# Expert slot lists from indicator products on TensorE, with the token table kept for overflow slots

## The reference, cut to what matters

```python
scores = jax.nn.sigmoid((t @ w_router).astype(jnp.float32))
_, eidx = lax.top_k(scores + router_bias.astype(jnp.float32), TOP_K_EXPERTS)   # 8 of 64 experts
g = jnp.take_along_axis(scores, eidx, axis=1)
g = g / jnp.sum(g, axis=-1, keepdims=True) * ROUTED_SCALE
...
def expert_block(args):
    e, toks, gs = args
    xb = t[toks]
    return swiglu(xb, w1[e], w3[e], w2[e]) * gs[:, None]
...
shared = swiglu(t, ws1, ws3, ws2)
return (routed + shared).reshape(B, S, D)
```

## Time and profile before

| | |
|---|---|
| median of 3 runs | 2526.91 us |
| profiled execution | 2550.12 us |
| its span | 2548.3 us |
| PE busy | 2292.6 us (90%) |
| DVE busy | 1565.9 us (61%) |
| ACT busy | 1190.4 us (47%) |
| POOL busy | 289.9 us (11%) |
| mean granted clock of PE | 0.949 of full speed |

### The profile page before, as it was taken

How to read it: one execution, slowest core, us unless ns; L and a number is a source line. 1 busy time by engine, 2 the same in 40 slices (tenths; PEclk the granted TensorE clock), 3 DMA queues, 4 the chain that set the end, 5 groups by cost and what they waited for, 6 DMA issues and landing times.

```text
span 2548.3 us, 31998 instructions
## 1 busy us (share of the span) xinstructions
PE 2292.6 (90%) x10228; PEld 1779.6 (70%) x10228; DVE 1565.9 (61%) x2404; ACT 1190.4 (47%) x1774; POOL 289.9 (11%) x345
## 2 busy tenths in 40 slices
PE   6998999399999999995399989999979878999997
PEld 4776677277777777774375768887868646888875
DVE  6789654489888888886765553332453566433334
ACT  4422433088888888884134433322231573333322
POOL 0000003322332332323400000000000000000000
PEclk8999997699999999998599999999999989999999
DMA  7521133399999999996520122223212101222222
GB/s 305 195 100 58 42 131 95 77 337 380 375 355 373 375 356 355 354 345 231 204 99 25 59 68 97 99 94 104 100 66 99 42 1 66 99 91 98 99 100 83
DMA packets 124602, 422.63 MB, mean 166 GB/s; under 512 B 21024, under 2 KB 21152, under 8 KB 124384
## 3 DMA queue, kind: packets, MB, share of 16 engines
q1 hardware_dynamic: 98176, 367.86, 40.6%
q0 software_dynamic: 25376, 50.66, 5.4%
q10 hardware_dynamic: 960, 2.97, 0.3%
HBM read 419.68 MB, written 39.47 MB: 180 GB/s over the span
## 4 chain that ended last, share of the span: by engine, by line
PE 59%; DMA 15%; DVE 12%; issue 5%; ACT 4%; DVEq 1%; POOL 1%; another core or an unknown queue 0%; SPq 0%; ACTq 0%; POOLq 0%
PE PS L283 17%; PE PS L285 16%; PE PS L284 16%; DMA eraw<-wstream 14%; DVE wl L191 3%; PE PS L628 3%; ACT wh L186 2%; PE PS L650 2%; POOL YG L2276 1%; PE PS L639 1%; DMA ada_w<-wada 1%; DVEq L1188 1%; DVE M L1185 1%; DVE X L555 1%; DVE X L559 1%
## 5 line engine op out<-in xcount | busy, mean ns | idle before, releaser
L191 DVE TENSOR_TENSOR wl<-raw,wh 128x1024 fp32r<-128x1024 f32 x239 | 292.6, 1225 | 402.9 <-ACT wh L186 389.8
L283 PE MATMUL PS<-HTh,wh 128*128 128x512 f32 x1248 | 503.4, 403 | 39.4 <-DVE HTl L581 18.7
L191 DVE TENSOR_TENSOR wl<-eraw,wh 128x1024 fp32r<-128x1024 f32 x384 | 460.1, 1225 | 82.8 <-ACT wh L186 72.1
L284 PE MATMUL PS<-HTl,wh 128*128 128x512 f32 x1248 | 491.4, 394 | 0.7 <-issue 0.7
L285 PE MATMUL PS<-HTh,wl 128*128 128x512 f32 x1248 | 491.3, 394 | 0.3 <-issue 0.3
L186 ACT ACTIVATE wh<-eraw 128x1024 fp32r<-128x1024 f32 x384 | 392.1, 1053 | 106.0 <-DMA eraw<-wstream 80.0
L186 ACT ACTIVATE wh<-raw 128x1024 fp32r<-128x1024 f32 x239 | 251.7, 1056 | 393.7 <-PE PS L285 371.4
L283 PEld LDWEIGHTS PS<-HTh,wh 128*128 128x128 f32 x1248 | 237.9, 191 | 105.3 <-issue 35.6
L284 PEld LDWEIGHTS PS<-HTl,wh 128*128 128x128 f32 x1248 | 238.1, 191 | 51.2 <-issue 3.8
L285 PEld LDWEIGHTS PS<-HTh,wl 128*128 128x128 f32 x1248 | 237.6, 190 | 51.7 <-issue 0.5
L283 PE MATMUL PS<-wh,XTh 128*128 128x512 f32 x536 | 223.0, 416 | 5.4 <-DVE XTl L1873 2.4
(11 more groups left out here) (403 smaller groups left out, 3491.9 us busy)
## 6 DMA issues: line engine op xcount, KB each, us to landing
eraw<-wstream SPq DMA_DIRECT2D x192, 1024.0 KB
raw<-wstream SPq DMA_DIRECT2D x240, 512.0 KB, 3.2
ada_w<-wada SPq DMA_DIRECT2D x24, 512.0 KB, 4.3
eraw<-wexp SPq DMA_DIRECT2D x9, 1024.0 KB
ada_wb<-wada SPq DMA_DIRECT2D x2, 2048.0 KB, 15.9
ada_g<-wada SPq DMA_DIRECT2D x2, 2048.0 KB, 10.6
X<-xT SPq DMA_DIRECT2D x4, 512.0 KB, 8.2
ada_w<-wada SPq DMA_DIRECT2D x1, 2048.0 KB, 23.7
```

The source lines that it names most:

```text
L191: nc.vector.tensor_tensor(wl[:, ci % RING, :], src, wh[:, ci % RING, :].bitcast(F32), ALU.subtract).then_inc(split_done, 1)
L283: nc.tensor.matmul(o, lh, rh, start=start, stop=False)
L284: nc.tensor.matmul(o, lh, rl, start=False, stop=False)
```

## The change

The slot lists of the first 128 slots of every expert no longer come from the table in memory. For each token block and choice, DVE builds two indicator matrices: `HOTS`, which is 1 where the token's rank in its expert is the slot number, and `HOTE`, which is 1 where the column is its expert, times the token number less 512. 32 matmuls on PE sum `HOTS` transposed times `HOTE` in PSUM, so that each slot of each expert holds its token number less 512, and 0 where it is empty. This work is hung between the chunks of the shared expert (`hot` after the second and third, `lists_pe` after the fourth, `lists_dve` and `list_rows` after the fifth and sixth), and `more_counts` and `more_blocks_of` move one chunk later.

The table remains for slots beyond 128. The scatters write only those: for all others the place is set beyond the table (`NOROW`), and a bounds check leaves them out. POOL issues the 32 scatters after the gathers of experts 0 to 3 and before that of expert 4; it reads the table back in step 0 and the list of blocks in step 1. DVE and PE turn it in steps 2 and 3. The 32 gate steps are spread over steps 0 to 3 and 60 to 63, four in each. SP no longer waits for the lists before it loads chunks 8 to 11, but for `more_blocks_of`.

The diff, cut to its core:

```diff
+            TOKM = place("TOKM", [P, NB], 11064)
+            R8 = place("R8", [P, NB, 8], 11072)
+            E8 = place("E8", [P, NB, 8], 11104)
+            RSB = place("RSB", [P, E], 11136)
+            LF = place("LF", [P, E], 11200)
+            SLOT = place("SLOT", [P, P], 20032)
+            HOTE = place("HOTE", [P, NB, 8, E], 8192)
+            HOTS = place("HOTS", [P, NB, 8, P], 4096)
+            TI2 = nc.alloc_sbuf_tensor_at("TI2", [P, 2, P], I32, offset=RSTD_AT)
+            TF2 = nc.alloc_sbuf_tensor_at("TF2", [P, 256], F32, offset=RSTD_AT + 4 * 256)
...
+                nc.vector.tensor_scalar(E8[:], POS8[:], 1.0 / S, -(S / 2 + 0.5) / S, ALU.mult, ALU.add)
                 dve.wait_ge(sem("ranks"), 2)
...
+                nc.vector.tensor_scalar(E8[:], R8[:], float(P), NOROW, ALU.is_le, ALU.mult)
+                dve.drain()
+                nc.vector.tensor_tensor(E8[:], E8[:], POS8[:], ALU.add)
+                dve.drain()
+                nc.vector.tensor_scalar(POSI[:], E8[:].rearrange("p a b -> p (a b)"), -1.0, None,
+                                        ALU.add).then_inc(sem("places"), 1)
+            def hot(dve, tbs):
+                dve.wait_ge(sem("h2_out"), 16)
+                for tb in tbs:
+                    nc.vector.tensor_tensor(HOTE[:, tb, :, :], POS[:, tb, :].unsqueeze(1).broadcast_to([P, 8, E]),
+                                            POS8[:, tb, :].unsqueeze(2).broadcast_to([P, 8, E]), ALU.is_equal)
+                    nc.vector.tensor_tensor(HOTS[:, tb, :, :], SLOT[:].unsqueeze(1).broadcast_to([P, 8, P]),
+                                            R8[:, tb, :].unsqueeze(2).broadcast_to([P, 8, P]), ALU.is_equal)
+                    dve.drain()
+                    nc.vector.tensor_scalar(HOTE[:, tb, :, :], HOTE[:, tb, :, :], TOKM[:, tb:tb + 1], None, ALU.mult)
+                    dve.drain().then_inc(sem("hot"), 1)
+            def lists_dve(dve):
+                dve.wait_ge(sem("listed"), 1)
+                nc.vector.tensor_scalar(slots(IDX)[:, :, 0], PS[:, 2, 0:E], float(S), None, ALU.add)
+                nc.vector.tensor_copy(LF[:], PS[:, 2, 0:E])
+                dve.drain().then_inc(sem("lists"), 1)
...
+            def list_rows(dve):
+                nc.vector.tensor_scalar(LF[:], LF[:], 0.0, NOROW, ALU.is_ge, ALU.mult)
+                dve.drain()
+                nc.vector.tensor_tensor(LF[:], LF[:], const("rows").rearrange("p (e r) -> p e r", r=4)[:, :, 0], ALU.add)
+                dve.drain()
+                nc.vector.tensor_tensor(LF[:], LF[:], RSB[:], ALU.add)
+                dve.drain()
+                nc.vector.tensor_copy(slots(YIX)[:, :, 0], LF[:])
+                dve.drain().then_inc(sem("lists"), 1)
...
-            def gate_places(dve):
...
+            def gate_place(dve, n):
+                tb, k = n // 8, n % 8
+                nc.vector.scalar_tensor_tensor(out=LF[:], in0=SCO[:, tb, :], scalar=POSC8[:, tb, k:k + 1],
+                                               in1=G[:, tb, :], op0=ALU.is_equal, op1=ALU.mult,
+                                               accum_out=GK[:, tb, k:k + 1])
+                dve.drain()
             @stage("pool")
             def _(pool):
                 pool.wait_ge(sem("empty"), 1)
                 pool.dma_start(table.rearrange("(p s) o -> p (s o)", p=P), TI[:].rearrange("p a b -> p (a b)")).then_inc(sem("table_dma"), 16)
                 pool.wait_ge(sem("table_dma"), 16)
+                pool.wait_ge(sem("h2_out"), 16)
+            def table_scatter(pool):
                 pool.wait_ge(sem("places"), 1)
                 for tb in range(NB):
                     for k in range(8):
                         pool.indirect_dma_start(
                             out=table, out_offset=bass.IndirectOffsetOnAxis(ap=POSI[:, tb * 8 + k:tb * 8 + k + 1], axis=0),
-                            in_=TOK[:, tb:tb + 1], in_offset=None).then_inc(sem("table_dma"), 16)
+                            in_=TOK[:, tb:tb + 1], in_offset=None, bounds_check=E * S - 1,
+                            oob_is_err=False).then_inc(sem("table_dma"), 16)
+            def table_back(pool):
                 pool.wait_ge(sem("table_dma"), 16 + 16 * NB * 8)
-                pool.dma_start(TI[:], table.rearrange("(a p s) o -> p a (s o)", p=P, s=P)).then_inc(sem("table_dma"), 16)
+                pool.dma_start(TI2[:], table.rearrange("(a p s) o -> p a (s o)", p=P, s=P)).then_inc(sem("table_dma"), 16)
+            def blocks_back(pool):
                 pool.wait_ge(sem("blocks"), 1)
                 pool.dma_start(blocks, TBI[:]).then_inc(sem("blocks_dma"), 16)
                 pool.wait_ge(sem("blocks_dma"), 16)
                 pool.dma_start(TB[0:1, :], blocks[0:36, :].rearrange("(o p) c -> o (p c)", o=1)).then_inc(sem("blocks_dma"), 16)
-                pool.wait_ge(sem("h2_out"), 16)
+            def table_pe(pe):
...
+                pe.wait_ge(sem("table_f"), 1)
+                for a in range(2):
+                    mm = nc.tensor.transpose(PS[:, 5, a * P:(a + 1) * P], TF2[:, a * P:(a + 1) * P], const("ident"))
+                mm.then_inc(sem("table_t"), 1)
...
+            def table_dve(dve):
+                dve.wait_ge(sem("table_t"), 1)
+                nc.vector.tensor_copy(slots(IDX)[:, :, 1:4], PS[:, 5, 0:256].rearrange("p (e r) -> p e r", r=4)[:, :, 1:4]
+                                      ).then_inc(sem("places"), 1)
+                nc.vector.tensor_scalar(TF2[:], PS[:, 5, 0:256], float(S), NOROW, ALU.is_ge, ALU.mult)
+                dve.drain()
+                nc.vector.tensor_tensor(TF2[:], TF2[:], const("rows"), ALU.add)
+                dve.drain()
+                for r in range(1, 4):
+                    v = slots(TF2)[:, :, r]
+                    nc.vector.tensor_tensor(v, v, RSB[:], ALU.add)
+                dve.drain()
+                nc.vector.tensor_copy(slots(YIX)[:, :, 1:4], slots(TF2)[:, :, 1:4]).then_inc(sem("places"), 1)
...
+                    hot(dve, (0, 1))
+                if c == 2:
+                    hot(dve, (2, 3))
                     more_counts(dve)
+                if c == 4:
+                    lists_dve(dve)
+                    more_blocks_of(dve)
+                if c == 5:
+                    list_rows(dve)
+            def lists_pe(pe):
+                for tb in range(NB):
+                    pe.wait_ge(sem("hot"), tb + 1)
+                    for k in range(8):
+                        mm = nc.tensor.matmul(PS[:, 2, 0:E], HOTS[:, tb, k, :], HOTE[:, tb, k, :],
+                                              start=tb + k == 0, stop=tb + k == NB + 6)
+                mm.then_inc(sem("listed"), 1)
+            def shared_pe(pe, c):
                 if c == 3:
-                    more_blocks_of(dve)
-
-            def shared_pe(pe, c):
-                if c == 2:
+                    lists_pe(pe)
+                if c == 3:
...
-            @stage("dve")
-            def _(dve):
-                gate_places(dve)
...
-            @stage("pe")
...
             @stage("sp")
             def _(sp):
-                sp.wait_ge(sem("places"), 3)
+                sp.wait_ge(sem("table_dma"), 16)
+                sp.wait_ge(sem("blocks"), 1)
                 for j in range(8, ER, 2):
...
+                    if n == 3:
+                        table_pe(pe)
                 steps(pe, prologue, step)
...
+                    if n == 2:
+                        dve.wait_ge(sem("table_dma"), 32 + 16 * NB * 8)
+                        nc.vector.tensor_copy(TF2[:], TI2[:].rearrange("p a b -> p (a b)")).then_inc(sem("table_f"), 1)
+                    if n == 3:
+                        table_dve(dve)
+                    if n < 4 or n >= E - 4:
+                        for j in range(4):
+                            gate_place(dve, 4 * (n if n < 4 else n + 8 - E) + j)
...
-                    pool.wait_ge(sem("places"), 2)
+                    pool.wait_ge(sem("lists"), 1)
                     for n in range(4):
+                        pool.wait_ge(h2_low, hl0 + 2 * n + 2)
                         gather(pool, n, 0)
-                    pool.wait_ge(sem("places"), 3)
+                    table_scatter(pool)
+                    pool.wait_ge(sem("lists"), 2)
                 def step(n, i):
                     if n + 4 < E:
                         gather(pool, n + 4, i)
                     elif n + 2 < E:
                         p = n + 4 - E
+                        pool.wait_ge(sem("places"), 3)
                         more_gather(pool, p, pool.value_load(TB[0:1, 3 * p + 1:3 * p + 2], min_val=0, max_val=255))
                     scatter(pool, n, i)
+                    if n == 0:
+                        table_back(pool)
+                    if n == 1:
+                        blocks_back(pool)
                 steps(pool, prologue, step)
```

More of the change, by code:

```diff
@@ L128, in build @@
         rstd = sb("rstd", [P, S])
+        RSTD_AT = nc.sbuf_base - 4 * S
         lamc = sb("lamc", [P, 8])
```

(58 more changed lines are left out.)

5 lines of the change are left out of this document (4 added, 1 removed).

## The result

The changed kernel takes 2539.16 us (median of 5 runs, 2531.67 to 2539.86) against 2526.18 (5 runs): ratio 1.0041, interval 1.0029 to 1.0052, 7 to 13 us slower. The forecast of 2535 had side and size, but its terms did not all come out: two errors of opposite sign nearly cancelled, which is luck.

What follows compares the result with a forecast made beforehand. Expert steps taken as bound by the weight stream, before 590 us by PE. Stream +3.6, following experts +3, tail +1.5 gave +8.1, 2535 us; range 2527 to 2543, widened to 2511 to 2545.

Steps and rivals of the forecast that it cites:

- Which time to sum against: Whole kernel: the 21.8 us of late signals belong to the profiled execution; timed runs have the first expert matmul near 490.0.
- rival of real late signals: Shared expert: late signals are real and vanish with the scatter, 21.8 us saved, 2513 us; chance 0.22.
- Shared expert: Shared expert: down product at 460.0, 6.2 us later than 453.8; list products hidden beside DVE's work.
- What that gain is: Before the experts: the gates' 11.7 us are gone; first expert matmul 10.4 us before 490.0.
- Scatters on POOL: POOL, between gathers 3 and 4: 32 scatters slowed by DVE's splits; gather 4 issued at 523.6.
- U: First expert matmul on PE: forecast at 479.6 us in the changed kernel, 490.0 in the kernel before.
- The conflict with VectorE: POOL's scatters in expert steps: DVE splits of two SBUF operands block them, ending 8.8 us later than without conflict.
- the first sentence that was taken from the Trainium skill: SBUF access: a VectorE instruction with two SBUF inputs and a GpSimd instruction reading SBUF block each other whole.
- the page's inference about descriptor generation: POOL's scatters: such a VectorE instruction leaves descriptor generation alone; by this the scatters end 8.8 us sooner.
- PE's stand: Step 2, before expert 4's transposes: PE stands 22 us for its gather, landing 6.5 us after issue.
- Stream: Weight stream in expert steps: +3.6 us from a full ring, then +3 (0 to 5) over five experts.
- Tail: Last four expert steps: gates need 1.5 us per step on DVE with 1.3 free; +1.5 us.

Runs made afterwards that it cites:

- second profile of the kernel before: The kernel before, unchanged, profiled once more: 2527.71 us.
- The gates alone: Kernel before with only the gate products moved, four to a step, into steps 0 to 3 and 60 to 63: 2529.91 us, ratio 1.0007.
- the two copies: Scatters before gathers 0 to 3, looped gates, chunks 8 to 11 first, plus two PSUM copies ahead of VectorE's last splits: 2516.91 us, ratio 0.9955.
- first profile of the kernel before: The kernel before, unchanged, the profile the prediction was made from: 2550.12 us.
- the scatters early: Changed kernel with the 32 table scatters back in front of POOL's gathers 0 to 3: 2524.9 us, ratio 0.9981.
- the gates are in the loop too: Changed kernel with scatters before gathers 0 to 3 and gate products one per step in steps 4 to 59: 2521.31 us, ratio 0.9963.
- moved to the loop: Gate products one per step in steps 4 to 59: in the changed kernel 2532.32 us; with scatters before gathers 0 to 3 as well, 2521.31 us.

## Why the prediction came out as it did

- **Which time to sum against: right, and it decided the side.** 490.0 was forecast for the first expert matmul in timed runs, 491.77 measured; silu and AFs came within 1.1 us of the forecast, the end of the shared expert 1.6 us behind it (467.0, 465.4). The rival of real late signals is out.
- **Shared expert: 1.4 us short.** The down product was to come 6.2 us later than before, at 460.0; it came at 462.67, 9.2 us later than in the second profile of the kernel before (453.45), and 1.6 of these were there at the shared expert's first matmul (426.80, 428.42). The 32 list products take 7.25 us, within the 4.1 to 7.8 bounded, but stand in PE's queue ahead of the down product until 462.31; and VectorE's next split ran at 458.92, not 456.4, so AHl was done at 462.26. Both end together, so the products cost nothing beside VectorE's work, as forecast. First expert matmul 482.39 against 479.6; the gain to there 9.4 us against 10.4, or 10.9 without the 1.5 us that were there at 384 us.
- **What that gain is: wrongly named.** I wrote that the gates' 11.7 us are gone. The gates alone, taken away, gave nothing at expert 0; it is the scatters' landing and the read-back that left the path.
- **Scatters on POOL: right in place, the time partly by luck.** Forecast: gather 4 issued at U + 44, 523.6; measured 521.90. U itself came 2.8 us later than forecast, so this is U + 39.5: the 32 scatters took 47.8 us (473.01 to 520.82), where the forecast had 51.7. The conflict with VectorE is there (0.98 to 1.97 us; shown by itself by the two copies), though no scatter took over 2 us, where several over 3 were forecast. The trace agrees with the first sentence that was taken from the Trainium skill (SBUF — State Buffer, "Who interferes with whom"), and not with the page's inference about descriptor generation.
- **PE's stand: 12.3 us, 22 forecast.** The gather landed 3.4 us after its issue, not 6.5: by then the stream had stopped (DMA share 0.16), a case for which the earlier trace rows has no row. And PE wanted it at 512.98, U + 30.6, not U + 28.5: 1.5 us had been taken off for the low clock at the start of the experts, but the changed kernel starts there too (0.63 to 0.67 us a matmul until 486 us, granted clock 0.83 from 480 to 490). The step of 9.4 us is right, but not from the rows named for it: 507.50 to 541.87 in four gives 8.6, and 9.4 is the distance from the third expert's transposes on (523.13 to 541.87 in two).
- **Stream: too dear.** +3.6 and +3 forecast; at expert 63 the changed kernel is 1.9 us behind, 0.4 if the 1.5 us of 384 us are taken off, 4.0 against the first profile of the kernel before set back by its 20.0 us at expert 0. All three are less than 6.6. It is 8.5 us ahead at expert 0, 2.2 behind after the hole, 7.8 behind at expert 7, 4.7 at 22 and 1.9 at 63: the stream makes up most of it. Of the way from expert 4 to 7 the forecast had next to nothing; gates were put "beside PE's stall", but those of steps 2 and 3 and the table lie behind it. With the scatters early and no hole, the same stretch loses 4.7 us, and 1.1 when the gates are in the loop too; what PE waits for there is VectorE's split.
- **Tail: too cheap, the term furthest off in proportion.** +1.5 forecast, +5.6 measured: 3.5 by the gates (as much as alone in the kernel before; moved to the loop they give back 2.7 and 3.8) and 2.1 by the last scatter behind VectorE's splits. A further 3.2 us lie behind the last gather of expert rows (1301.1 us to the end before, 1304.3 after); that stretch has the same code and varies from 1299.7 to 1304.7 over the twelve traces, so it is not put down to the change.

8.1 us were forecast; the timed runs give 13.0 by their medians, and the two spans 10.3, as 1.9 + 5.6 + 3.2 less 0.4 in the gathers of expert rows. Of these, 1.5 and 3.2 us lie in code that the change leaves alone, so this pair of profiles puts only 5.6 us on the change; where the rest of the timed 13 us lies is open. That the hole is the largest part is shown by the timed runs themselves, since the early scatters take 15 us off. The stream was 3 to 6 us too high and the tail 4 too low, and that the sum came close owes something to luck.

## What to carry to other kernels

Work that is moved off a critical path into a queue must be counted by what stands behind it in that queue: here 32 small scatters cost nothing in front of the first gather, whose readers are busy until 478 us, and 11 to 15 us in front of the fifth. Before a removed step is credited with its length, look for what else ended at the same time: the gates' 12 us lay under a landing. When one profile is far from the median of the runs, take another before any sum. And before two profiles are compared stage by stage, look at how far they are apart before the first edited line: here up to 2.2 us at 384 us.

## What was not expected of the hardware

- 32 table scatters, the last issued at 468.19 us (0.96 us each), are all landed only at 477.1, after a wait of 8.0 us; in the version with the gates moved the wait is 9.7 us, in the first profile of the kernel before 4.7.
- A GpSimd scatter that starts 0.23 us behind a VectorE subtraction of two SBUF operands takes 1.85 us, one that starts 0.12 us ahead of it 1.00. With the landing behind it, that is 2.1 us between the changed kernel and the one before at the end of the experts.
